# TensorE's middle MLP passes without a loop, a mask product in fp32r, and a norm summed on VectorE

## The reference, cut to what matters

```python
def squared_relu_mlp(h, w_up, w_down):                 # layers 0 and 1
    a = jax.nn.relu(jnp.einsum('bld,df->blf', h, w_up))
    return jnp.einsum('blf,fd->bld', a * a, w_down)
...
# gated_delta_rule: decay between places i >= j of one chunk of a head
decay = jnp.where(incl, jnp.exp(jnp.where(incl, diff, 0.0)), 0.0)
...
# second_block: norm, then gated feed-forward
f = swiglu(rms_norm(h, norm_pre_ffn[layer]), w_ffn_in[layer], w_ffn_out[layer])
```

## Time and profile before

| | us |
|---|---|
| median of 3 runs | 1946.34 (1943.33 to 1952.83) |
| the profiled execution | 1952.76 |
| its span, first to last instruction | 1951.0 |
| TensorE's matmuls busy | 1907.3 (98%) |
| VectorE busy | 1020.9 (52%) |
| ScalarE busy | 774.4 (40%) |

### The profile page before, as it was taken

How to read it: one execution, slowest core, us unless ns; L and a number is a source line. 1 busy time by engine, 2 the same in 40 slices (tenths; PEclk the granted TensorE clock), 3 DMA queues, 4 the chain that set the end, 5 groups by cost and what they waited for, 6 DMA issues and landing times.

```text
span 1951.0 us, 28914 instructions
## 1 busy us (share of the span) xinstructions
PE 1907.3 (98%) x11580; PEld 1672.4 (86%) x11580; DVE 1020.9 (52%) x1459; ACT 774.4 (40%) x1257; POOL 32.4 (2%) x31
## 2 busy tenths in 40 slices
PE   7999999999999999999999999999999999999997
PEld 7888789999989999888888877787899888888886
DVE  5654485654434455544444567778547353333435
ACT  5355442432222345423232434535676442212232
POOL 0100000100000000000000000000000000000000
PEclk9999999999999999999999999999999999999999
DMA  5221102233223232333333322222103223233321
GB/s 188 67 65 44 57 1 66 88 95 95 87 77 98 87 94 91 108 97 89 95 97 97 94 90 87 76 66 84 56 1 109 77 87 97 87 91 104 97 87 54
DMA packets 47187, 162.36 MB, mean 83 GB/s; under 512 B 5368, under 2 KB 7672, under 8 KB 46936
## 3 DMA queue, kind: packets, MB, share of 16 engines
q1 hardware_dynamic: 46208, 158.60, 26.4%
q10 hardware_dynamic: 856, 2.00, 0.3%
HBM read 156.38 MB, written 4.19 MB: 82 GB/s over the span
## 4 chain that ended last, share of the span: by engine, by line
PE 93%; DVE 3%; ACT 2%; DVEq 1%; issue 1%; DMA 0%; SPq 0%; ACTq 0%
PE ps L465 80%; PE ps L1056 2%; PE ps L927 1%; PE ps L597 1%; PE ps L1076 1%; PE ps L903 1%; PE ps L905 1%; PE ps L1061 0%; PE ps L1000 0%; PE ps L572 0%; ACT WU L2071 0%; PE ps L573 0%; PE ps L1187 0%; PE ps L1216 0%; PE ps L1206 0%
## 5 line engine op out<-in xcount | busy, mean ns | idle before, releaser
L465 PE MATMUL ps<-UH,whi 128*128 128x264 f32 (+2 forms) x1904 | 646.9, 340 | 14.5 <-DVE wlo L2372 9.7
L465 PE MATMUL ps<-UL,whi 128*128 128x264 f32 (+2 forms) x1904 | 638.1, 335 | 1.0 <-issue 1.0
L465 PE MATMUL ps<-UH,wlo 128*128 128x264 f32 (+3 forms) x1616 | 522.7, 323 | 0.0
L1537 ACT ACTIVATE whi<-raw 128x1024 fp32r<-128x1024 f32 x282 | 295.8, 1052 | 436.1 <-PE ps L465 415.5
L465 PEld LDWEIGHTS ps<-UH,whi 128*128 128x128 f32 x1904 | 359.4, 189 | 56.4 <-issue 17.0
L465 PEld LDWEIGHTS ps<-UL,whi 128*128 128x128 f32 x1904 | 359.4, 189 | 39.5 <-issue 2.4
L2372 DVE TENSOR_TENSOR wlo<-raw,whi 128x1024 fp32r<-128x1024 f32 x248 | 308.3, 1246 | 47.3 <-ACT whi L1537 35.7
L465 PEld LDWEIGHTS ps<-UH,wlo 128*128 128x128 f32 (+1 forms) x1616 | 304.7, 189 | 25.5 <-issue 1.1
L465 PE MATMUL ps<-HH,whi 128*128 128x264 f32 (+1 forms) x768 | 246.4, 321 | 0.0
L465 PE MATMUL ps<-HL,whi 128*128 128x264 f32 (+1 forms) x768 | 246.4, 321 | 0.0
L465 PE MATMUL ps<-HH,wlo 128*128 128x264 f32 (+1 forms) x768 | 245.7, 320 | 0.0
(11 more groups left out here) (463 smaller groups left out, 2369.6 us busy)
## 6 DMA issues: line engine op xcount, KB each, us to landing
raw<-W SPq DMA_DIRECT2D x284, 512.0 KB, 3.6
H<-xT SPq DMA_DIRECT2D x4, 528.0 KB, 6.8
spill<-H SPq DMA_DIRECT2D x1, 2048.0 KB, 8.9
H<-spill SPq DMA_DIRECT2D x1, 2048.0 KB, 9.2
MEM<-memT ACTq DMA_DIRECT2D x1, 1024.0 KB, 4.7
out<-H SPq DMA_DIRECT2D x2, 512.0 KB, 2.9
out<-H SPq DMA_DIRECT2D x4, 256.0 KB, 3.2
masks<-masks SPq DMA_DIRECT2D x1, 768.0 KB, 9.9
```

Of the source, the lines that this page charges most:

```text
L465: mm = pe.matmul(dst, a, b, start=start and n == 0, stop=stop_ and n == 2)
L1537: act.activation(whi[s % NB][:, :, :], raw[s % NB][:, :, :], ACT.Copy).then_inc(w_hi, 1)
```

## The change

TensorE's loop over the two middle quarters is replaced by straight code, in both layers. The mask product of `decay` reads fp32r copies of identity and `future`, which ScalarE makes once, after the gates' inputs are there. For the feed-forward's norm ScalarE squares each half of the tokens into a buffer of its own, VectorE adds its eight tiles to one, and TensorE makes one product with ones for each half. Both products stand after the fifth step of half 1's third tile. Two weight splits move earlier on VectorE and one on ScalarE.

```diff
-                loop(FQ - 2, 128, 16, lambda i: quarter(i + 1))
-                quarter(FQ - 1)
+                for q in range(1, FQ):
+                    quarter(q)
...
                 if j == 0:
+                    pe.wait_ge(N["exact"], 1)
                     pe.wait_ge(N["l2_r"], 4)
...
-                pe.matmul(ps[:, b, :].rearrange("p (x t) -> p x t", x=4), ident,
-                          future.rearrange("p (a t) -> p a t", a=1).to_broadcast([P, 4, P]), start=True, stop=False,
+                pe.matmul(ps[:, b, :].rearrange("p (x t) -> p x t", x=4), IDR[:, :],
+                          FUR[:, :].rearrange("p (a t) -> p a t", a=1).to_broadcast([P, 4, P]), start=True, stop=False,
...
             def input_norm(x):
-                pe.wait_ge(sq_done, squares_before(6) + 2 * x + 2)
-                for k in range(KT):
-                    mm = pe.matmul(ps[:, 6 + x, 0:NMEM], ones, SQB[:, k, :], start=k == 0, stop=k == KT - 1)
-                mm.then_inc(sq_summed, 1)
+                pe.wait_ge(sq_added, sum(ADDS[:6]) + x + 1)
+                pe.matmul(ps[:, 6 + x, 0:NMEM], ones, SQB[x][:, 0, :], start=True, stop=True).then_inc(sq_summed, 1)
...
+                        if (x, e, k) == (1, 2, 4):
+                            input_norm(0)
+                            input_norm(1)
...
-                    if (x, e) in ((0, 2), (1, 0)):
-                        input_norm(x)
...
             act.wait_ge(N["ab_x"], 1)
+            act.activation(IDR[:, :], ident, ACT.Copy)
+            act.activation(FUR[:, :], future, ACT.Copy).then_inc(N["exact"], 1)
...
             def input_squares(x):
-                if x:
-                    act.wait_ge(sq_summed, sum(SUMS[:6]) + 1)
...
             weights_hi(0, to=FFN_SLOT + 3)
+            weights_hi(0, to=FFN_SLOT + 4)
             input_squares(0)
-            weights_hi(0, to=FFN_SLOT + 4)
...
+            def input_sum(x):
+                a = SQB[x]
+                dve.wait_ge(sq_done, squares_before(6) + 2 * x + 2)
+                for n in (4, 2, 1):
+                    dve.drain()
+                    last = dve.tensor_tensor(a[:, 0:n, :], a[:, 0:n, :], a[:, n:2 * n, :], ALU.add)
+                last.then_inc(sq_added, 1)
...
             input_lo(0, 1)
+            weights_lo(0, to=FFN_SLOT + 3)
             dve.wait_ge(r_ready, 7)
             residual_half(1, 0)
-            weights_lo(0, to=FFN_SLOT + 3)
+            weights_lo(0, to=FFN_SLOT + 4)
             residual_half(1, 1)
-            weights_lo(0, to=FFN_SLOT + 4)
             input_lo(1, 0)
             input_lo(1, 1)
+            input_sum(0)
+            input_sum(1)
             dve.wait_ge(r_ready, 8)
```

More of the change, by code:

```diff
@@ L100, in last_tile @@
     return next(t for t, end in enumerate(END_OF) if end >= SLOT * (slot + 1))
-ADDS = [7, 7, 6, 7, 6, 7, 0, 6]
+ADDS = [7, 7, 6, 7, 6, 7, 2, 6]
 SUMS = [1, 1, 1, 1, 1, 2, 2, 1]
@@ L240, in build @@
                                ("ABL", [P, KT, 16], FR))
+        IDR, FUR = region(AB0, ("IDR", [P, P], FR), ("FUR", [P, P], FR))
         MEM, MSQ, MH, ML, RM, VM = region(
@@ L288, in build @@
         OMH, = region(END - 8192, ("OMH", [P, HEADS, SEQ], FR))
-        Y, SQB = region(S0 + 16 * SEQ * 4, ("Y", [P, KT, L], F32), ("SQB", [P, KT, NMEM], F32))
+        Y, SQB0, SQB1 = region(S0 + 16 * SEQ * 4, ("Y", [P, KT, L], F32), ("SQB0", [P, KT, NMEM], F32),
+                               ("SQB1", [P, KT, NMEM], F32))
+        SQB = [SQB0, SQB1]
         FH, FL, FO, GA0, GA1, GS0, GS1, GC0, GC1 = region(
@@ L323, in build @@
         N = {n: sem(n) for n in ("mem_sq", "mem_sum", "mem_r", "mem_hi", "mem_lo", "mem_vt", "mem_vtc", "pool_v",
-                                 "conv", "conv_silu", "ab", "ab_row", "ab_in", "ab_hi", "ab_lo", "ab_x", "ab_ln", "ab_g", "ab_exp",
+                                 "conv", "conv_silu", "ab", "ab_row", "ab_in", "ab_hi", "ab_lo", "ab_x", "exact", "ab_ln", "ab_g", "ab_exp",
                                  "l2_sq", "l2_sum", "l2_r", "l2_done", "ma_s", "ma_o",
@@ L448, in _ @@
             class Stream:
-                pos, tile, slots, tiles = 0, 0, 0, 0
+                pos, tile = 0, 0
             st = Stream()
@@ L456, in take @@
                 if b == 0:
-                    pe.wait_ge(w_lo, s + 1 + st.slots)
+                    pe.wait_ge(w_lo, s + 1)
                 st.pos += 1
@@ L466, in passes @@
                 return mm
[L468 to L477, removed]
             def tile(ks, n, xh, xl, m=P, before=None, mid=None, read=None):
                 t = st.tile
-                pe.wait_ge(evac[t % 2], t // 2 + FREE + st.tiles // 2)
+                pe.wait_ge(evac[t % 2], t // 2 + FREE)
                 dst = psum(t, n, m)
@@ L2275, in input_squares @@
             def input_squares(x):
-                if x:
-                    act.wait_ge(sq_summed, sum(SUMS[:6]) + 1)
                 for y in range(2):
-                    act.activation(SQB[:, 4 * y:4 * y + 4, :], H[:, 4 * y:4 * y + 4, part(x)], ACT.Square).then_inc(sq_done, 1)
+                    act.activation(SQB[x][:, 4 * y:4 * y + 4, :], H[:, 4 * y:4 * y + 4, part(x)], ACT.Square).then_inc(sq_done, 1)
             half_out(0, 6)
```

## The result

| | median us | runs | lowest to highest |
|---|---|---|---|
| before | 1950.76 | 12 | 1943.33 to 1952.83 |
| changed | 1939.76 | 12 | 1935.72 to 1941.47 |

Ratio 0.9941, 95% interval 0.993 to 0.9952: 11 us less, between 9 and 14. The forecast was 1930, 1924.5 to 1938.5. The direction was right, the time lies 9.8 us above the forecast and 1.3 above the range.

What follows compares the result with a forecast made beforehand. TensorE, busy 98% of the span, was taken to bound the kernel. Gains of 7.7 + 5.0 + 3.8 = 16.5 us from 1946.3 gave 1929.8, said as 1930, range 1924.5 to 1938.5.

Steps and rivals of the forecast that it cites:

- Part 1: TensorE's loops over the middle quarters: written out, layer 0's edge stops no more, saving 7.7 us, bounds 0 and 9.
- The three losses of the earlier trace: At layer 0's loop edge: a first stop of 3.92 us, a second of 1.32 and a slow clock costing 2.5.
- Rival A: Layer 0's edge: the stop is smaller or absent without the profiler; gain 8.8 us, time 1937.5; chance 0.13.
- Part 1, layer 1's edge: Layer 1's loop: nothing is lost at its edge, and fetching the written-out second pass is hidden; gain 0 us.
- D: Layer 1's edge stops in most executions, the profiled one was lucky; up to 7.7 us more gain, 1922; chance 0.04.
- E: Layer 1's written-out pass stops for four code blocks, 4.3 us each, 17.3 in all; slower, 1947; chance 0.02.
- Part 2: Mask product of the eight decay groups: one fp32r pass takes 0.23 us instead of 0.86, saving 5.0 us.
- Rival C: Mask or norm brings nothing because VectorE or ScalarE move behind TensorE later; time 1935; chance 0.05.
- Part 3: Feed-forward's norm: 6.0 us less TensorE work, less a new stop of 2.3 before tile 4; net 3.8 us.
- Folds, arrival, chain and stop: Before tile 4: folds ready 0.5 us early, TensorE arrives at 1584.1, chain of 6.2 us, wait 2.3 to 1586.4.
- rival B: New stop before tile 4 is worse: clock falls or folds are late, price about 2.5 us; 1932.5; chance 0.12.
- The base, 1946.34: Whole kernel: median of the three runs shown, from which the profiled execution's gain of 16.5 us was subtracted.

Runs made afterwards that it cites:

- e9_pad16: Kernel before, both loops kept, with 16 more wait instructions in TensorE's code of layer 0's first quarter, shifting the code behind: 1951.61 us, ratio 0.9999.
- e2_mask: Kernel before with only the fp32r copies and the mask product in fp32r: 1946.50 us, 5.1 less, ratio 0.9978.
- e10_pad236: Kernel before, both loops kept, with 236 more wait instructions in TensorE's code of layer 0's first quarter: 1946.82 us, 5.7 less, ratio 0.9969.
- e5_keep1: Changed kernel with layer 1's loop kept and layer 0's written out: 1938.41 us, 14.1 less than the kernel before, ratio 0.9923.
- e1_loops: Kernel before with only TensorE's two loops written out as straight code: 1945.52 us, 6.0 less, ratio 0.9968.
- e13_after: The changed kernel itself, timed again in a later series on another chip: 1937.82 us, 13.8 less than the kernel before, ratio 0.9927.
- e8_small: Changed kernel with four small loops in layer 0's middle quarters in place of straight code: 1936.22 us, 15.4 less than the kernel before, ratio 0.9924.
- e12_order: Changed kernel with VectorE emptying tile 2 right behind tile 0, before tile 1: 1938.68 us, 13.0 less than the kernel before, ratio 0.9929.
- e11_split: Changed kernel with tile 4's weights split before the norm's factor instead of after it: 1936.57 us, 15.1 less than the kernel before, ratio 0.9921.

## Why the prediction was wrong

- **Part 1, 7.7 us: right in place, and by the medians too large by 1.7** (6.0 alone, with an interval that reaches 8.4). The three losses of the earlier trace rows were those of one execution, and I carried them over whole. In the padded kernel, whose ten runs all look like stopping ones, the profiled edge lost 2.4 + 2.3 us and a stretch at the lower clock, 5.9 in all; in an execution that doesn't stop, the edge loses nothing. Rival A, which said so, had 0.13; for the median execution it was wrong, since 33 of 40 stop. My reason for the edge (in the prediction's words, "the edge lies in the code, and the fetch must happen each time") was false: e2_mask and e10_pad236 have the edge and no fetch.
- **What I took for the cause needed a size.** The Trainium skill ("Runtime: NRT & Kernel Launch", Instruction fetch mechanics) says that PE's instruction memory is 128 KiB, 2048 instructions, filled in blocks of 256; a few lines on it says that only two blocks are held. By the first, as an estimate from that page's figures, layer 0's body (768 matmuls are 1536 instructions with their weight loads, and 35 more) is 6.1 of 8 blocks and may just fit with what is fetched ahead; layer 1's (384 matmuls) is 3.1 and fits easily. The runs agree with the first and speak against the second: both bodies were run again without one fetch (e10_pad236, e5_keep1). A block of 256 agrees too: e1_loops fetched 12 for 190 us of straight code, some 1570 matmuls and as many loads. In the prediction I had weighed only the second.
- **Part 1, layer 1's edge, 0 us: right** (e5_keep1), and rivals D and E, which hung on it, are out: written out, four more blocks are fetched and the chain's piece stays 311.5 us.
- **Part 2, 5.0 us: right** (e2_mask 5.1; 0.23 us in the trace). Rival C is out.
- **Part 3, 3.8 us: the working was right, the price of the stop was not.** Folds, arrival, chain and stop came out to a tenth: 2.3 forecast, 2.35 measured, and tile 4 starts 1590.16 - 1573.95 = 16.2 us earlier than before, where 12.4 had been gained up to the feed-forward (1557.68 to 1545.32 by TensorE's last YH product), so 3.85. But the stop also slowed the clock for some 3.4 us, 1.6 us more, so that the trace leaves 2.2; alone the part measured 1.7. This was rival B at 0.12. I held against it that the stop is shorter than the 3.8 us after which the clock was seen to fall; that bounds nothing below 3.8. The step that failed is that I priced a new idle time at its length and put the clock behind it at nothing.
- **The base, 1946.34: too low by 4.4.** The sum was right for the profiled pair to 2.3 us (16.5 forecast, 14.2 measured; nearly all the rest is the slow window, 1.6, and a start 0.5 us later). I took it from a median of three runs that twelve runs moved to 1950.76, although the profile itself had said 1952.76. This step failed in its mechanism too. Among the 40 runs above the lowest that belongs to a stopping group is 1948.90, so two of the three runs, 1946.34 and 1943.33, very likely had no stop (their clock was not recorded, so this is not shown). I then took a stop of 7.7 us from a base that had none: for the base, rival A was right, and its argument for itself (the profile lies "6.4 above the median, nearly the stop's price") was the sign.
- **The account.** Of the 9.9 us between 1929.8 and 1939.76, 4.4 are this base and 5.5 the gain, by the medians 1.7 in part 1, 2.1 in part 3, and 1.7 within what two measurements of the same pair differ by. The gain measured 11.0 (9.4 to 13.7) in the result and 13.8 (11.5 to 17.0) in e13_after; the second does not exclude 16.5. Either correction alone would have put the time inside the range: 1950.8 - 16.5 = 1934.3, or 1946.3 - 11 = 1935.3.
- **The range was narrower than its own bounds.** "1926 to 1935, from the bounds of part 1 and part 3" leaves out the 0 of part 1: with it and a stop of 4 us the gain is 0 + 5.0 + 2.1, and the upper end 1939.2.

What stays open: which of two equal executions of the kernel before stops at the edge. Its code stands at the border, and I have no row that shows what tips it. Also what decides the clock after a stop: before tile 4 it fell in six of seven profiled executions with 1.8 to 2.35 us of idling, and not in e8_small's, with 2.35; the last section has a shorter stop that did it as well.

## What to carry to other kernels

Writing a loop out gained here for a body of 1571 instructions and not for one of 803, and for the large one a shift of its code was worth as much as writing it out; look in the instruction queue for the body's second pass before paying for it. A step that leaves the critical path and returns as a later wait is worth its length less the wait, and on TensorE less the slow clock that may follow the wait (1.6 us here); putting what the next tile needs ahead of the late factor took both away. And what one execution lost may be taken only from a base whose executions lost it too; three runs do not show that.

## What the runs showed of the hardware

- TensorE ran a loop body of 1571 instructions again without fetching any of it, in 30 us of unbroken work around the edge (e10_pad236), and with 220 fewer instructions ahead of it the same edge cost 5.9 us in the profiled execution (e9_pad16).
- A taken branch by itself costs TensorE nothing that the trace shows, at 0.12 us from matmul to matmul (e8_small).
- The length of an idle time does not by itself decide the clock. Before tile 4 1.84 us was followed by 3.3 us at the lower clock (e12_order), 0.99 us was not (e11_split), and 2.35 us once was not (e8_small). A stop of 1.11 us in layer 0, 237 to 241 us into the span and of the same length in all 14 profiled executions (the kernel before, the changed one and the twelve runs), was followed by the lower clock in seven of them, e11_split among them; it is part of why equal executions differ. The rows are e8_small's tile 4, then e11_split's stop of 1.11 us:

```profile
1572.80 0.50 PE L468 MATMUL ps<-UH,whi 128*128 128x512 f32 x1 [2.35 <-DVE GA L3169]
...
1572.80:1576.20 3.40, 3.40 (x15) 2.78 (x16) 2.27 (x3) 3.03 (x4) 0.00 (x0) 1.00 0.66 187
...
237.03 0.55 PE L564 MATMUL ps<-MF,LTH 128*128 128x512 f32 x1 [1.11 <-ACT XE L1694]
...
237.30:240.30 3.00, 3.00 (x8) 1.97 (x6) 1.66 (x13) 1.71 (x4) 0.00 (x0) 0.50 0.00 0
```

- The spread of one kernel's runs goes in part with the clock: of the changed kernel's twelve, the fastest (1935.72) had a mean granted clock of 0.997, the slowest three (1940.43 to 1941.47) 0.994, the other eight 0.995, and those still span 1938.18 to 1940.38.
